# A fused attention and PEER layer on one core: 96 gathered tokens in kinds of 64 and 32 for 88 in kinds of 64, 16 and 8

## The reference

```python
q = (hc @ wq).reshape(T, PEER_HEADS, 2, PEER_KEY_DIM)          # 8 heads, two halves of 128
s1 = jnp.einsum('thd,hnd->thn', q[:, :, 0], sub_keys[:, 0])    # 128 keys per half
s2 = jnp.einsum('thd,hnd->thn', q[:, :, 1], sub_keys[:, 1])
v1, i1 = lax.top_k(s1, 16)
v2, i2 = lax.top_k(s2, 16)
cand = (v1[..., :, None] + v2[..., None, :]).reshape(T, PEER_HEADS, 256)
sc, ci = lax.top_k(cand, 16)
e = take(i1, ci // 16) * 128 + take(i2, ci % 16)               # expert numbers
g = jax.nn.softmax(sc, axis=-1)
act = gelu(jnp.einsum('td,thkd->thk', hc, exp_u[e]))
return jnp.einsum('thk,thkd->td', g * act, exp_v[e])
```

## Time and profile before

| | |
|---|---|
| time, median of 3 runs | 846.58 us (844.03 to 846.83) |
| profiled execution, its own time | 847.16 us |
| its span, first to last instruction | 845.4 us |
| PE busy | 819.9 us, 97% |
| DVE / ACT / POOL busy | 560.8 / 171.8 / 208.6 us |
| moved by DMA | 286.39 MB, 339 GB/s over the span |
| TensorE clock granted, mean | 0.994 |

### The profile page before, as it was taken

One profiled execution on the slowest core, in us unless ns is written; L12 is line 12 of the kernel. 1 busy time (PEld: TensorE's weight loads), 2 busy tenths in 40 slices (PEclk: granted clock), 3 DMA queues, 4 the chain that ended last, 5 costly groups with the idle time before them and its releaser, 6 DMA issues.

```text
span 845.4 us, 14556 instructions
## 1 busy us (share of the span) xinstructions
PE 819.9 (97%) x5758; PEld 783.5 (93%) x5758; DVE 560.8 (66%) x1134; ACT 171.8 (20%) x449; POOL 208.6 (25%) x216
## 2 busy tenths in 40 slices
PE   6999999999989999999999999999999999999996
PEld 4998879888979999999999999989999999999996
DVE  4959889698994998688788898554553344343302
ACT  4454575542111112121111111000000000000003
POOL 2000000000104321655434436533222323322100
PEclk9999999999999999999999999999999999999998
DMA  9998781653898998999999999999999999999951
GB/s 336 405 373 333 328 371 78 274 187 114 226 273 276 411 409 290 382 408 409 409 393 365 361 393 377 410 408 409 409 409 409 378 408 391 389 388 398 342 174 50
DMA packets 75909, 286.39 MB, mean 339 GB/s; under 512 B 9483, under 2 KB 11707, under 8 KB 74562
## 3 DMA queue, kind: packets, MB, share of 16 engines
q1 hardware_dynamic: 48482, 191.00, 59.1%
q0 software_dynamic: 27360, 94.47, 29.6%
HBM read 283.90 MB, written 1.52 MB: 338 GB/s over the span
## 4 chain that ended last, share of the span: by engine, by line
PE 86%; DMA 7%; DVE 5%; ACT 1%; issue 1%; ACTq 0%; SPq 0%; DVEq 0%
PE banks L1223 35%; PE banks L1194 32%; DMA raw<-in_u_t 3%; PE banks L941 3%; PE banks L1206 2%; PE banks L859 2%; PE banks L894 2%; PE banks L937 2%; DMA raw<-in_w_mod 2%; DMA raw<-in_v_b 2%; PE banks L1010 1%; PE banks L864 1%; DVE sc_w L1330 1%; PE banks L910 1%; PE banks L1242 1%
## 5 line engine op out<-in xcount | busy, mean ns | idle before, releaser
L1223 PE MATMUL banks<-act,raw 128*128 128x168 f32 x2048 | 306.1, 310 | 0.4
L1223 PEld LDWEIGHTS banks<-act,raw 128*128 128x128 f32 x2048 | 294.8, 191 | 10.4 <-DMA raw<-in_v_b 10.4
L1194 PE MATMUL banks<-hT,raw 128*128 128x168 f32 x2048 | 298.4, 307 | 3.2 <-DMA raw<-in_u_t 3.1
L1194 PEld LDWEIGHTS banks<-hT,raw 128*128 128x128 f32 x2048 | 292.3, 190 | 4.7 <-DMA raw<-in_u_t 4.7
L1696 DVE SCALAR_TENSOR_TENSOR row_sums<-rows,weight,row_sums 128x1024 f32<-128x1024 f32 x85 | 109.2, 1285 | 142.7 <-DMA rows<-in_v_b,idx 124.0
L541 POOL DMA_INDIRECT rows<-in_u_rows,idx x88 | 109.4, 1243 | 128.1 <-DVE dots L1673 91.7
L541 POOL DMA_INDIRECT rows<-in_v_b,idx x88 | 86.2, 980 | 179.7 <-PE banks L1223 142.5
L1673 DVE CUSTOM_DVE_ANT_0 rows<-rows,h_rows 128x1024 f32<-128x1024 f32 x88 | 105.9, 1221 | 18.7 <-issue 13.4
L791 ACT ACTIVATE turned<-banks,ccol 128x256 f32<-128x256 f32 x8 | 3.8, 473 | 293.6 <-PE banks L1223 293.6
L749 ACT ACTIVATE act<-banks 128x168 f32<-128x168 f32 (+20 forms) x121 | 33.1, 273 | 121.5 <-PE banks L1194 114.8
L508 POOL DMA_DIRECT2D h_lines<-h_stage x1 | 0.5, 541 | 211.4 <-ACT h_stage L774 211.4
(11 more groups left out here) (238 smaller groups left out, 825.5 us busy)
## 6 DMA issues: line engine op xcount, KB each, us to landing
raw<-in_u_t SPq DMA_DIRECT2D x128, 512.0 KB
raw<-in_v_b SPq DMA_DIRECT2D x128, 512.0 KB
wq<-in_wq SPq DMA_DIRECT2D x2, 4096.0 KB, 18.2
sh_w<-in_w_mod SPq DMA_DIRECT2D x8, 512.0 KB, 13.2
sc_w<-in_w_mod SPq DMA_DIRECT2D x8, 512.0 KB, 13.4
win<-in_w_in SPq DMA_DIRECT2D x8, 512.0 KB, 14.1
win<-in_w_in SPq DMA_DIRECT2D x1, 4096.0 KB, 20.8
sc_w<-in_w_mod SPq DMA_DIRECT2D x2, 2048.0 KB, 23.4
```

The source lines that it names most:

```text
L1194: last = nc.tensor.matmul(dst, raw[n % RAW][:, c * P:(c + 1) * P], hT[:, c, 0:MANY], start=(c == 0), stop=(c == DC - 1))
L1223: return nc.tensor.matmul(chunk_place(c)[:, 0:MANY], raw[(BLOCKS + j) % RAW][:, c * P:(c + 1) * P], act[:, j, :], start=(j == 0 and c < 4) ...
```

## The change

- `KINDS = (64, 32)`: 96 tokens are gathered, 160 are dense. Gathers are 96 + 96, gate groups are 20, blocks multiply 160 columns, and `few_sums` has two kinds.
- **h2 of the gathered tokens.** PE transposes it before block 2, after all scores have left PSUM. The first kind's `h2_rows` are filled by two copies of 64 rows from `h2_stage` in SBUF to `h2_rows[0]`, on SP's queue behind loads 9 and 11. The second kind's come from `h2_lines` in HBM, replicated four times, on SP's queue behind load 58; POOL still writes `h2_lines`.
- **Expert numbers.** They are written and spread by SP, behind loads 25 and 26, each after a wait of SP. POOL goes from `h2_lines` straight to waiting for `idx`, and then to the gathers.
- **Order on PE.** The last key scores follow block 0 instead of preceding it; `query_banks` and its waits are changed for that.
- **Sort.** `part` is kept with each value doubled, so that the comparison with `place_h` has pairs as its innermost dimension. Dots between sort steps are always up to two, 24 in all.
- **Numbers.** `EARLY` 24, `EXP_AT` 54, `TURN_AT` 60, `GATE_AT` 65 (last group at block 122), `PACE` 1.36.

```diff
-KINDS = (64, 16, 8)
+KINDS = (64, 32)
...
-EARLY = 18
+EARLY = 24
...
-H2_AT = 4
-EXP_AT = 50
+H2_AT = 2
+H2_FIRST = (9, 11)
+H2_LATER = (58,)
+EXPERTS_OUT = 25
+EXPERTS_IN = 26
+EXP_AT = 54
 SORT_SKIP = 2
-TURN_AT = 55
-GATE_AT = 60
+TURN_AT = 60
+GATE_AT = 65
...
-PACE = 1.45
+PACE = 1.36
...
-        part = at("part", 13312 + 1280, [P, 2, HEADS, TOPK], F16)
+        part = at("part", 13312 + 1280, [P, 2, HK, 2], F16)
...
+        h2_in, h2_late, idx_in = (loaded[n] for n in ("sh2a", "g1b", "g1a"))
...
-        H2_SAVED, H2_IN, EXPERTS_SAVED, IDX_IN, FEW_SAVED, FEW_IN = 16, 64, 80, 128, 144, 192
+        FEW_SAVED, FEW_IN = 16, 16 + 16 * len(KINDS)
+
+        def lines_of(lines, kind):
+
+            count = KINDS[kind]
+            return bass.AP(tensor=lines, offset=KIND_AT[kind] * HK, ap=[[count, P // count], [HK, count], [1, count]])
...
-            return (6, 2, 4)[(g - 2) % 3]
+            return (6, 4, 2)[(g - 2) % 3]
...
+                if n in H2_FIRST:
+                    half = H2_FIRST.index(n) * KINDS[0]
+                    sp.wait_ge(xn_ready, TT + 3)
+                    sp.dma_start(h2_rows[0][half:half + KINDS[0], :], h2_stage[0:KINDS[0], :]).then_inc(h2_in, 16)
+                if n in H2_LATER:
+                    kind = 1 + H2_LATER.index(n)
+                    count = KINDS[kind]
+                    sp.wait_ge(h2_saved, 16)
+                    sp.dma_start(h2_rows[kind][:, :],
+                                 bass.AP(tensor=h2_lines, offset=KIND_AT[kind] * D,
+                                         ap=[[0, P // count], [D, count], [1, D]])).then_inc(h2_late, 16)
+                if n == EXPERTS_OUT:
+                    sp.wait_ge(chosen_ready, 1)
+                    sp.dma_start(expert_lines.ap(), e_u[FEW0:P, :]).then_inc(idx_in, 16)
+                if n == EXPERTS_IN:
+                    sp.wait_ge(idx_in, 16 + 16)
+                    for kind in range(len(KINDS)):
+                        sp.dma_start(idx[:, KIND_AT[kind]:KIND_AT[kind + 1]], lines_of(expert_lines, kind)
+                                     ).then_inc(idx_in, 16)
...
             pool.wait_ge(xn_ready, TT + 3)
-            pool.dma_start(h2_lines.ap(), h2_stage[0:FEW, :]).then_inc(lines_moved, 16)
-            pool.wait_ge(lines_moved, H2_SAVED)
-            for n, count in enumerate(KINDS):
-                pool.dma_start(h2_rows[n][:, :],
-                               bass.AP(tensor=h2_lines, offset=KIND_AT[n] * D, ap=[[0, P // count], [D, count], [1, D]])
-                               ).then_inc(lines_moved, 16)
-
-            def spread_lines(dst, lines):
-
-                for n, count in enumerate(KINDS):
-                    pool.dma_start(dst[:, KIND_AT[n]:KIND_AT[n + 1]],
-                                   bass.AP(tensor=lines, offset=KIND_AT[n] * HK,
-                                           ap=[[count, P // count], [HK, count], [1, count]])).then_inc(lines_moved, 16)
-
-            pool.wait_ge(chosen_ready, 1)
-            pool.dma_start(expert_lines.ap(), e_u[FEW0:P, :]).then_inc(lines_moved, 16)
-            pool.wait_ge(lines_moved, EXPERTS_SAVED)
-            spread_lines(idx, expert_lines)
-            pool.wait_ge(lines_moved, IDX_IN)
+            pool.dma_start(h2_lines.ap(), h2_stage[0:FEW, :]).then_inc(h2_saved, 16)
+
+            pool.wait_ge(idx_in, 16 + 16 + 16 * len(KINDS))
             for i in range(GATHERS):
...
-                    spread_lines(gate_few, gate_lines)
+                    for kind in range(len(KINDS)):
+                        pool.dma_start(gate_few[:, KIND_AT[kind]:KIND_AT[kind + 1]], lines_of(gate_lines, kind)
+                                       ).then_inc(lines_moved, 16)
...
-                if g == 4:
+                if g == 3:
...
-                if g in QUAD_AFTER:
+                if g in QUAD_AFTER[:-1]:
                     key_scores(QUAD_AFTER.index(g))
...
+                if n == 0:
+                    pe.wait_ge(q_sum, LISTS // 2 - 3)
...
                 if n == H2_AT:
+                    pe.wait_ge(s_out, TT * LISTS // 4)
...
                 u_block(n)
+                if n == 0:
+                    key_scores(len(QUAD_AFTER) - 1)
...
                 if i == 0:
-                    ve.wait_ge(lines_moved, H2_IN)
+                    ve.wait_ge(h2_in, 16 + 16 * 2)
+                if i == KINDS[0]:
+                    ve.wait_ge(h2_late, 16 + 16 * len(H2_LATER))
...
                 if places[0] > SORT_SKIP and dotted[0] < EARLY:
-                    some_dots(min(2 - places[0] % 2, EARLY - dotted[0]))
+                    some_dots(min(2, EARLY - dotted[0]))
...
-                link(nc.vector.tensor_copy(part[:, :, :, :], part_u[:, :, :, :]))
+                link(nc.vector.tensor_copy(part[:, :, :, :], spread(part_u[:, :, :, :].rearrange("p n h k -> p n (h k)"), 3, 2)))
                 for half in range(2):
 
-                    place = spread(spread(place_h[:, :], 1, TOPK), 1, HEADS)
-                    link(nc.vector.tensor_tensor(hit[:, :, :, :], spread(part[:, half], 3, TOPK), place,
-                                                 ALU.is_equal))
+                    place = spread(place_h[:, :].rearrange("p (q two) -> p q two", two=2), 1, HK)
+                    link(nc.vector.tensor_tensor(hit[:, :, :, :].rearrange("p h k (q two) -> p (h k) q two", two=2),
+                                                 spread(part[:, half], 2, TOPK // 2), place, ALU.is_equal))
```

More of the change, by code:

```diff
@@ L293, in hybrid_peer_layer @@
             sem, ("second_ready", "onehot_ready", "gates_ready", "gates_used", "gates_out"))
-        lines_moved = sem("lines_moved")
+        lines_moved, h2_saved = map(sem, ("lines_moved", "h2_saved"))
         gathered = [sem(f"gathered{n}") for n in range(SLOTS)]
```

## The result

| | before | changed |
|---|---|---|
| time, median of 4 runs | 846.71 us | 841.58 us (839.74 to 841.98) |
| ratio | | 0.9936, 95% interval 0.9915 to 0.9958 |
| profiled execution / its span | 847.16 / 845.4 us | 841.98 / 839.9 us |
| moved by DMA | 286.39 MB | 294.30 MB |

The changed kernel is faster by 0.64%, where 830 us, 2%, had been forecast. The time lies outside 820 to 838, to which the prediction gave 0.67, and inside the wider 820 to 843.

The account below looks back on a forecast made before the run. The prediction took DMA (409 GB/s) and PE to bound the kernel by turns, DMA setting V after the change. U -11.7, V -2.5, `few_sums` -2.0 and last blocks -0.4 gave -16.6 us, so 830 us, range 820 to 838 (0.67).

Parts of the forecast that it names:

- PE's terms: PE in U and the end: shorter blocks -13.7 us, gate group -0.9, key scores -1.5, load waits -3.1, `few_sums` -2.0, last blocks -0.4.
- SyncE's part: SP writes expert numbers at 248.8 us, first gather at 257 (262 at the upper end), no load stall charged (0 to 3).
- The late h2 load: Second kind's replicated load behind load 58 in U: costs 1.0 us, between 0 and 5.
- The 4.5 us for the sort: U from 258 to about 330 us: denser gathers leave 228 GB/s for loads, 2.30 us a block; costs 4.5 us (0 to 10.3).
- the 2.0 for the gate stage: U's 20 gate groups: DMA sharing gives three loads in 7.67 us, PE wants 7.49; costs 2.0 us (0 to 3.8).
- The catch-up in V: Start of V: 49 blocks at 2.557 us under equal sharing until gathers are back at pace, V changing by -2.5 us.
- 12.8: Gathers made up in V by the kernel before, 38 shared blocks at 0.31 each and one more; reused for the changed kernel.
- 291.2: Forecast length in us of V until `few_sums`, against 293.7 before.
- The second way: Cross-check by bytes: 218 MB from 257 us take 533 us, ending at 790, `few_sums` at 802; the chain gives 803.6.
- PE stays the bound: Rival for U and V: U falls by 19.2 us, V to 280.7, in all -34.6, giving 812 us; chance 0.07.
- The gathers never catch up: Rival in V: 106 blocks share equally at 2.557 us, V 310.3 us, total 849 or 855 us; chance 0.07.
- A stall on the queues: Rival in U: SP's wait or the replicated load starves PE, equal sharing before 330 adds 6; 838 to 844 us; chance 0.14.

Follow-up runs that it names:

- Experiment 4: Changed kernel with the second kind's replicated h2 load kept whole but issued behind load 15 instead of 58: 836.42 us, ratio 0.9895.
- the split: Changed kernel with the late h2 load cut into four loads of 32 partitions, same bytes, place and time: 835.30 us, ratio 0.9866.
- experiment 10: Kernel before with only the kinds (64, 32) and pace 1.36, the rest of the change left out: 843.38 us, ratio 0.9964.
- experiments 7: Changed kernel with the late h2 load in four, plus four more dots while DVE waits for the transposed keys: 835.26 us, ratio 0.9882.
- experiment 8: Changed kernel with the late h2 load in four, gates three blocks sooner, and one dot a block in the gate stage: 832.82 us, ratio 0.9839.
- experiment 9: Changed kernel with the late h2 load in four and the sort's dots as before the change, 18 in all: 838.75 us, ratio 0.9911.

## Why the prediction was wrong, and where it was right

**PE's terms were right.** A U block takes 2.19 us. The wait for the last query sum is gone, and so are the four waits at 241 to 252. `few_sums` takes 3.49 us, 2.6 less where 2.0 was said, by estimate 0.9 of it through the clock of the kernel before. The comparison takes 1.22 us instead of 2.29:

```profile
238.29 1.22 DVE L1764 TENSOR_TENSOR hit<-part,place_h 128x2048 f16<-128x2048 f16 x1
```

**SyncE's part was right.** The write went out at 249.08 (said 248.8), the first gather at 257.86 (said 257), and no load was late for it.

**The late h2 load was mis-sized.** The step "Three such loads cost 3.1 us; I take a third, 1.0, between 0 and 5" was the first that failed: cut into four, the load gave back 6.3 us. A third of an old cost was the wrong measure, since the old loads ran while no gather was under way, and this one runs where loads and gathers had shared the engines for 70 us. Experiment 4 bears this out: the same load ahead of the gathers gives 836.4 us. The rule of the Trainium skill that was set beside it ("DMA: Bandwidth & Descriptors", Why a DMA increments its semaphore by 16 and not by 1), four engines for this shape and an estimated 5.1 us, came closer in size. The trace agrees in that the same bytes in loads of 32 partitions raise 283 GB/s to 341 and remove the wait. It does not bear the rule out as the whole reason: from 334 to 340 the share of the engines is 0.97 and 1.04 at 207 and 220 GB/s. Nor did the 1.02 at 226 GB/s of the kernel before, which the prediction read as a few slow engines, since a share of 1.02 takes all sixteen. Without this load U would have been as forecast: with the split V begins 12.4 us sooner than before. The forecast without its 1.0 for the load was 12.7. The 4.5 us for the sort and the 2.0 for the gate stage were not measured one by one. In the sort, 31 blocks took 73.52 us, 2.37 each for 2.30 said, which is 5.6 us above 2.19 a block; with the split, the gate stage lost nothing from its first group on.

**The catch-up in V was mis-sized, and this is the larger error.** The step reads: "Those 38 made up 0.31 gathers each, and the first nine one more, 12.8. With 1.36 a shared block makes up only 0.265, so 49 are needed." It took over the 12.8 of the kernel before. But 15 dots instead of 7 were still to be done when V began, since eight dots were added, six of them in the sort, while the rate of five dots in six blocks stayed, and the last gates moved from block 120 to 122: behind them DVE has five blocks of U left instead of seven. Eight more owed at 0.265 each would make 30 blocks more; measured were 70 blocks at 2.56 instead of 49, 21 more. POOL's rows show the same debt: when V began, 7 gathers of u were still to be issued, none in the kernel before, and the issues were back at their pace 27 blocks of V later than before (50 for 23). The 21 blocks are 21 x (2.557 - 2.222) = 7.0 of the 9.6 us by which V came out longer than 291.2. The first eight blocks, at 2.34 for 2.18, give 1.3, the tail, at 2.23 for 2.222 and 2.18, another 0.6. In the prediction the dots late in the gate stage were seen as a relief for U ("DVE's dots hold the gathers to 5 in 6 blocks late in the stage"), and their price in V was left out.

**The second way had the same hole.** It let 218 MB flow at 409 GB/s without a gap. From 258 to 800 us the changed kernel moved 398. 542 us x 11 GB/s are 6.0 MB, or 14.6 us at 409, left unused, nearly all of it before V.

**The rivals.** "PE stays the bound" is out: the kernel whose gathers were left at 88 reached 827, not 812. "The gathers never catch up" named the right mechanism with 106 blocks for the measured 70. "A stall on the queues" had its place too, at the late load. Both belonged into the forecast itself, at part of their price.

**Luck at the end.** In the profiled spans U came out 4.7 us and V 9.5 us worse than forecast, 14.2 together. The span missed by only 11.1, since behind the start of `few_sums` 5.5 us were gained for the 2.4 forecast, mostly by the clock that had fallen there in the kernel before. In the three traces whose `few_sums` has three kinds it fell for about 7 us; in the ten with two kinds it fell for about 3.4 us in three and not at all in seven. Whether the kinds do this is not tested.

**What is shown and what is not.** That the late load in one piece costs 6.3 us, that work moved out of V shortens V (over the changed kernel and the eight variants of it with its kinds, V falls from 307.9 to 292.7 us as the dots in V fall from 21 to 5, some 0.95 us each), and that moving it costs U something, are measured. The count of dots is a measure within these variants only, as experiment 10 shows. That 14.4 us lie between the kernel with shorter matmuls alone and the changed one is measured, and V alone is 17.3 us longer; that the 16 gathers cause it is an inference, since the two kernels also differ in the pace, in the late loads and in `few_sums`, and no run has 96 gathers with another pace. Whether another order of loads and gathers could pass 832.7 us with this DMA traffic stays open.

## What to carry to other kernels

When two resources are near full, count what each stage leaves undone, and carry that as a debt into the next; a debt taken over from the old kernel is wrong as soon as the number of items or the engine that works them off has changed. It pays to try a replicated load as several plain ones, and to measure its price where the queues are full. A cut in the bound engine's work is worth only as much as the second resource can follow: 16.1 us came from the shorter matmuls alone, and the kernel that also gathers for the 8 tokens is 14.4 us slower than the one that leaves them out. And when two traces are compared, their granted clocks should be compared first, stretch by stretch.

## What the runs showed of the hardware

- One DMA of 512 KB whose source repeats four times and four DMAs of 128 KB with the same bytes differ by 6.3 us of kernel time at block 58 (841.6 and 835.3). Whole, but ahead of the gathers, the load costs hardly anything in time (836.4), though it still makes PE wait 1.41 us. Behind the whole load the engines' share is 0.97 to 1.04 at 207 to 220 GB/s for six us, half the rate at which they run at the same share elsewhere (409).
- Loads from SP and gathers from POOL, both with work waiting, share the engines equally again and again: six blocks in 15.36 us, 2.56 each, over 70 blocks at 409 GB/s. That is the same figure as in the kernel before, though the matmuls of a block had become 0.1 us shorter.
- In two kernels, experiments 7 and 8, the time did not move though 5 us changed places between U and V. In experiment 8 the earlier stage was itself at 408 GB/s with DVE at 94.5%; where it was at 372 (experiment 9), the work left undone there cost 3.5 us.
- The granted clock fell to the lower level behind a wait of PE of 3.01 us (0.50 from 343.80 to 347.20, one block 4.12 us for 2.34), and in the kernel before also without a wait, at the end of `few_sums` (0.51 from 822 to 829, one block 4.68 us for 2.26).
